# A decoder step with PEER experts on one core: top-16 lists taken in the query stage, gates placed earlier, and each gate placed by two single-pass products

## The reference, cut to what matters

```python
qry = einsum('td,de->te', xb, w_query)             # 1024 -> 8 heads x 2 halves x 128
s = einsum('thjd,jkd->thjk', qry, keys)            # 16 lists of 128 scores for each token
s_top, i_top = top_k(s, 16)                        # the best 16 of each list
cand = s_top[..0..][:, None] + s_top[..1..][None]  # sums of pairs, of one head
best, pos = top_k(cand, 16)                        # the best 16 sums: 16 experts a head
gates = softmax(best)
act = gelu(einsum('thkd,td->thk', peer_u[idx], xb))
out = einsum('thk,thkd->td', gates * act, peer_v[idx])
```

## Time and profile before

| | |
|---|---|
| median of three runs | 2429.15 us (2427.97 to 2431.12) |
| the profiled execution: its own time | 2427.98 us |
| its span | 2426.2 us |
| TensorE busy | 2295.1 us, 95% of the span |
| VectorE busy | 1560.2 us, 64% |
| ScalarE busy | 893.0 us, 37% |
| GpSimd busy | 882.0 us, 36% |
| transfers | 392.73 MB, mean 162 GB/s |

### The profile page before, as it was taken

How to read it: one execution, slowest core, us unless ns; L and a number is a source line. 1 busy time by engine, 2 the same in 40 slices (tenths; PEclk the granted TensorE clock), 3 DMA queues, 4 the chain that set the end, 5 groups by cost and what they waited for, 6 DMA issues and landing times.

```text
span 2426.2 us, 34102 instructions
## 1 busy us (share of the span) xinstructions
PE 2295.1 (95%) x12935; PEld 1956.2 (81%) x12935; DVE 1560.2 (64%) x3461; ACT 893.0 (37%) x1175; POOL 882.0 (36%) x428
## 2 busy tenths in 40 slices
PE   5999999868998999999989999999999999999998
PEld 4998899746648888888778888888888888888886
DVE  4766579464713158888889997786565555555552
ACT  3434455561122143323335554455332222222221
POOL 1333246154524337557510210000454444444441
PEclk9999999987998999999999999999999999999999
DMA  7221122646645255555546897586664555445540
GB/s 272 70 88 55 57 73 70 187 142 198 202 175 134 81 135 143 145 142 141 134 126 187 255 266 204 160 234 186 239 237 179 207 200 198 176 187 207 191 155 35
DMA packets 307412, 392.73 MB, mean 162 GB/s; under 512 B 14545, under 2 KB 257637, under 8 KB 302914
## 3 DMA queue, kind: packets, MB, share of 16 engines
q1 hardware_dynamic: 212162, 302.86, 40.3%
q10 hardware_dynamic: 91664, 75.54, 9.5%
q0 software_dynamic: 3456, 12.58, 1.6%
HBM read 305.70 MB, written 81.26 MB: 159 GB/s over the span
## 4 chain that ended last, share of the span: by engine, by line
PE 59%; DVE 3%; POOL 2%; issue 0%; ACT 0%; DMA 0%; DVEq 0%; ACTq 0%; POOLq 0%
PE bank L2597 29%; PE bank L2052 25%; PE bank L2548 4%; POOL utL_hid L2035 2%; DVE work L2271 1%; DVE work L2272 1%; PE bank L2553 1%; PE bank L2538 1%; DVE utL_hid L2042 0%; DVE ut_hid L2022 0%; DVE work L1980 0%; DVE work L1964 0%; POOL work L1964 0%; DVE work L2426 0%; PE bank L2617 0%
## 5 line engine op out<-in xcount | busy, mean ns | idle before, releaser
L2052 PE MATMUL bank<-pH,utH_hid 128*128 128x512 f32 x1024 | 406.1, 397 | 4.5 <-POOL utL_hid L2035 4.5
L2052 PE MATMUL bank<-pH,utL_hid 128*128 128x512 f32 x1024 | 400.0, 391 | 0.0
L2052 PE MATMUL bank<-pL,utH_hid 128*128 128x512 f32 x1024 | 400.0, 391 | 0.0
L2597 PE MATMUL bank<-area,work 128*128 128x512 f32 x1536 | 350.8, 389 | 0.0
L2597 PEld LDWEIGHTS bank<-area,work 128*128 128x128 f32 x1536 | 288.4, 188 | 59.7
L2209 POOL TENSOR_TENSOR work<-work,work 128x1024 fp32r<-128x1024 f32 x64 | 155.8, 2436 | 368.5 <-ACT work L2456 368.5
L2035 POOL TENSOR_TENSOR utL_hid<-ut_hid,utH_hid 128x1024 fp32r<-128x1024 f32 x66 | 182.5, 2767 | 175.8 <-PE bank L2052 147.7
L864 PE MATMUL ps_in<-hH_in,wH_in 128*128 128x260 f32 x816 | 237.4, 291 | 2.4 <-DVE projarea L915 1.4
L2370 DVE TENSOR_TENSOR utL_hid<-u_hid,utH_hid 128x512 fp32r<-128x512 f32 x64 | 147.5, 2305 | 135.3 <-ACT utH_hid L2460 135.3
L864 PE MATMUL ps_in<-hL_in,wH_in 128*128 128x260 f32 x816 | 231.8, 284 | 0.0
L864 PE MATMUL ps_in<-hH_in,wL_in 128*128 128x260 f32 x816 | 231.5, 284 | 0.0
(11 more groups left out here) (533 smaller groups left out, 4470.6 us busy)
## 6 DMA issues: line engine op xcount, KB each, us to landing
u_hid<-in_peer_u_dram SPq DMA_DIRECT2D x256, 256.0 KB, 5.0
work<-in_peer_v_dram SPq DMA_DIRECT2D x64, 1024.0 KB, 4.8
hidden_dram<-ge_hid ACTq DMA_DIRECT2D x64, 512.0 KB, 2.7
gates_dram<-area ACTq DMA_DIRECT2D x16, 2048.0 KB, 12.2
wb_in<-in_w_in_dram SPq DMA_DIRECT2D x26, 1024.0 KB, 5.1
wstage<-in_w_ada_dram SPq DMA_DIRECT2D x32, 512.0 KB, 5.0
area<-hidden_dram SPq DMA_DIRECT2D x16, 1024.0 KB
area<-gates_dram SPq DMA_DIRECT2D x16, 1024.0 KB
```

The costliest lines, as they stand in the source:

```text
L2052: mm = self.nc.tensor.matmul(self.pa[u % 2][:, :], w[:, k, :], x[:, k, :], start=(n == 0), stop=(n == 3 * KD - 1))
L2597: mm = nc.tensor.matmul(bank[k], v[s][:, j, cols], w[s][:, j, :], start=(start and x == 0), stop=(stop and x == 2))
```

## The change

It has four parts.

1. **Scores and lists move into the query stage.** After query product n TensorE scores list n-2 (4 float32 matmuls, `score`), from a copy that ScalarE now makes of each product (`evict`); ScalarE keeps the scores (`keep`), and VectorE takes the lists 0 to 12 of all four tiles there (`best_of_list`). `LATE` = 3 lists are left for units 0 to 5. The sub keys are loaded at the start of the query stage, and the first pair of expert rows at its middle; VectorE transposes that pair there.
2. **GpSimd does nothing for the units any more.** All 128 `move_low` and all picks are VectorE's.
3. **The selection of a tile has 11 steps** (`steps_by_unit`): in units 6 to 21 one step a unit, from 22 to 76 one in every second unit. Quads start in unit 19: one a unit up to 84, then 62 quads over the 37 units from 85 to 121.
4. **A gate is a rounded high part and a rest.** VectorE's one-hot carries the high part; ScalarE multiplies it by the ratio of rest to high part (`low_hots`), and TensorE adds two float32r products (`place`) where there was one float32 product. Step 10 of the selection computes the ratio, and a fourth row of `res` and `S.sel` carries it.

```diff
+            def evict(n):
+                act.wait_ge(q["product"], n + 1)
+                if n >= QR:
+                    act.wait_ge(q["scored"], n - QR + 1)
+                A_(halves(qry[n % QR]), ps[n % 2][:, :, 0:HN], ACT.Copy)
+                A_(S.qs[:, n % 2, n // 2, :], ps[n % 2][:, 1, T - HN:HN], ACT.Copy).then_inc(q["evicted"], 1)
+            def keep(n):
+                act.wait_ge(q["scored"], n + 1)
+                A_(S.lists[n], quad[n % 2], ACT.Copy).then_inc(q["kept"], 1)
             for n in range(2, CHUNKS):
                 move_high(n)
+                evict(n - 2)
+                if n >= 3:
+                    keep(n - 3)
                 if n == 3:
                     act.wait_ge(q["s_turned"], 1)
                     A_(halves(rows[:, :]), pt[0:B, :, :], ACT.Copy).then_inc(q["s_row"], 1)
+            for n in range(CHUNKS - 2, CHUNKS):
+                evict(n)
+                keep(n - 1)
+            keep(CHUNKS - 1)
...
+                    for a in range(4):
+                        sp.dma_start(S.hu[0][32 * a:32 * a + 32, :, :], S.uv[a, :, 0:8, :]).then_inc(q["first_in"], 16)
...
-            for n in range(CHUNKS):
-                dve.wait_ge(q["product"], n + 1)
-                V.tensor_copy(halves(qry[:, n, :]), ps[n % 2][:, :, 0:HN]).then_inc(q["evicted"], 1)
+            for n in range(CHUNKS - LATE):
+                dve.wait_ge(q["kept"], n + 1)
+                best_of_list(V, own, S.lists[n], S.wk, S.top[:, :, n, :], S.idx[:, :, n, :], range(NC))
...
+            def low_hots(q):
+                act.wait_ge(m["hot"], q + 1)
+                for t in range(4):
+                    last = nc.scalar.activation(oh[q % OH][:, 2, t, :], oh[q % OH][:, 0, t, :].bitcast(F32), ACT.Copy, scale=S.sel[:, 3, 4 * q + t:4 * q + t + 1])
+                last.then_inc(m["hot_low"], 1)
...
             def place(q):
-                pe.wait_ge(m["hot"], q + 1)
+                pe.wait_ge(m["hot_low"], q + 1)
...
                 for t in range(4):
-                    mm = nc.tensor.matmul(quad[q % 4][:, t, :], oh[q % OH][:, 1, t, :], oh[q % OH][:, 0, t, :], start=True, stop=True)
+                    for x in (0, 2):
+                        mm = nc.tensor.matmul(quad[q % 4][:, t, :], oh[q % OH][:, 1, t, :], oh[q % OH][:, x, t, :], start=(x == 0), stop=(x == 2))
...
             for u in range(UNITS):
-                if FIRST_DVE <= u + 1 < UNITS:
-                    H.move_low_dve(dve, u + 1)
+                if u + 1 < UNITS:
+                    H.move_low(dve, u + 1)
                 for q in QUADS[u]:
                     one_hots(q)
-                if u + 3 < UNITS and QUADS[u]:
+                if u + 3 < UNITS:
                     H.turn(dve, u + 3)
+                if u < 2 * LATE:
+                    l = 2 * PH - LATE + u // 2
+                    best_of_list(V, own, S.lists[l], S.wk, S.top[:, :, l, :], S.idx[:, :, l, :], range(2 * (u % 2), 2 * (u % 2) + 2))
+                if u in STEP:
+                    select(*STEP[u])
```

More of the change, by code:

```diff
@@ L1725, with best_of_list, query_phase @@
 UNITS = NKEY
-def query_phase(nc, A, S, XH, XL, hT, qry, PH_, PL_, buffers, sample_rows, first):
+def best_of_list(V, own, src, wk, top, idx, tiles):
+    for half in range(2):
+        at = slice(8 * half, 8 * half + 8)
+        of = wk if half else src
+        for t in tiles:
+            last = V.max(top[:, t, at], of[:, t, :])
+        own(last)
+        for t in tiles:
+            last = V.max_index(idx[:, t, at], top[:, t, at], of[:, t, :])
+            if not half:
+                last = V.match_replace(wk[:, t, :], top[:, t, at], src[:, t, :], LOW)
+        own(last)
+def query_phase(nc, A, S, XH, XL, hT, PH_, PL_, buffers, sample_rows, first):
     per = 2
@@ L1735, in query_phase @@
     BY_POOL = (2, 4, 5, 7)
+    QR = 3
+    qry = [carve(S.work, AT_OH + N * i, (P, N)) for i in range(QR)]
+    keys = carve(S.work, AT_OH + N * QR + 8, (P, 2, P))
     with Phase(nc) as ctx:
-        sb = lambda n, s: ctx.enter_context(nc.sbuf_tensor(f"{n}_query", s, F32))
         sem = ctx.sem
@@ L1825, in _, with score @@
             mm.then_inc(q["s_sum"], 1)
+            pe.wait_ge(q["keys_in"], 16)
+            nc.tensor.transpose(pk[:, 0:P], keys[:, 0, :], S.ident[:, :])
+            nc.tensor.transpose(pk[:, P:2 * P], keys[:, 1, :], S.ident[:, :]).then_inc(q["keys_t"], 1)
+            def score(n):
+                pe.wait_ge(q["evicted"], n + 1)
+                if n == 0:
+                    pe.wait_ge(q["keys_s"], 1)
+                if n == 1:
+                    pe.wait_ge(q["s_scaled"], 1)
+                if n >= 2:
+                    pe.wait_ge(q["kept"], n - 1)
+                for t in range(NC):
+                    mm = nc.tensor.matmul(quad[n % 2][:, t, :], qry[n % QR][:, t * L:(t + 1) * L], S.keysT[:, n % 2, :], start=True, stop=True)
+                mm.then_inc(q["scored"], 1)
             for n, h in [(0, 0), (1, 0), (0, 1), (1, 1)] + [(n, h) for n in range(2, CHUNKS) for h in range(2)]:
```

335 lines of the change are left out of this document (161 added, 174 removed).

## The result

| kernel | median us | range us | runs |
|---|---|---|---|
| before | 2429.1 | 2428.0 to 2431.1 | 4 |
| changed | 2468.0 | 2461.1 to 2478.8 | 4 |

The medians differ by 38.9 us, 1.6%. The recorded ratio, 1.0145 with a 95% interval of 1.0116 to 1.0175, is not quite the ratio of the medians (1.0160), but its interval holds it: the change costs some 35 to 39 us. The forecast was 2423 us with a range up to 2446, so both sign and range are missed. The profiled one took 2461.09 us, the fastest of the four; its span is 33.1 us above that of before (2426.2).

The account below looks back on a forecast made before the run. TensorE was taken as the bound nearly to the end. Query end 0.8, less 16.4 won, plus 9.0 new waits and 0.4 transposes gave -6.2 us: 2428.0 to 2421.8, median 2423, range 2408 to 2446.

Parts of the forecast that it names:

- the last sentence of part 4: Quads: ScalarE's four multiplications take about 1 us a quad on an engine busy half the time; no cost added.
- the part is worth nothing on TensorE: Quads: two float32r products give eight records like one float32 product, both bound by weight loads, 0.89 us; no gain.
- price of a record: Quads on TensorE: each record takes 0.111 us, set by its weight load, for float32 and float32r alike.
- cheap weight loads: Rival for the quads: weight loads do not bind float32r products, so about 2383 us; chance 0.06.
- four passes: Rival for the quads: narrow float32r products take float32's four passes, so about 2518 us; chance 0.12.
- Query end: Last query products to first unit: 19.0 + 2 + 2.5 = 23.5 us against 22.7, so 0.8 us slower.
- the weights of product 8: Query stage: weights land late behind the rearranging and expert rows; TensorE waits 1 to 6 us, taken as 2.
- 2.5 us of half clock in unit 0: First hidden unit: pauses behind score 15 lower TensorE's clock, losing 2.5 us (0 to 2.7).
- The early gates, the lists and VectorE: Lists hidden at 5.1 us against 6.6; VectorE falls behind in units 20 to 22, then pairs fit, 12.0 against 12.7.
- Backlog: VectorE's late one-hots make TensorE wait in units 21 to 23 and near the sample steps: 9 us of new waits.
- The forecast's terms for this stage: Hidden stage: 16.4 us of waits and half clock won, 9.0 of new waits, 0.4 for four more transposes.
- the 16.4 us that TensorE could win: Hidden stage: 13.7 us of waits for one-hots and GpSimd's rests plus 2.7 lost at half clock, all removable.

Follow-up runs that it names:

- the moved rows: Changed kernel, with SyncE issuing the four loads of the first expert rows behind the fifth pair of query weights instead of ahead of it: 2467.9 us.
- the version with all three edits: Changed kernel with one float32 product a gate, hidden-row and gate stores issued by SyncE, and first expert rows loaded behind the fifth pair of query weights: 2421.9 us.

## Why the prediction was wrong

**The step that failed** is the last sentence of part 4: "ScalarE's four multiplications a quad: 0.31 us each with overlap 0.2 to 0.3, about 1 us, on an engine busy for half of the time", costed at nothing. The length was near (four take 1.28 us, not 1), and the busy share was right (43%). What was not asked is whether ScalarE is always there to do them. It issues transfers as well, and the trace of before showed what that can take. Busy time does not count it, since an engine held in an issue is shown as idle. Moving the stores away gave 19.7 us of the hidden stage back, and 21 us of the median.

**The second term** is the same part's "the part is worth nothing on TensorE". Its price of a record held: eight records are 0.89 and 0.90 us as forecast, and the rivals of cheap weight loads and of four passes are both out. That it is the weight loads that set it was read from rows of before; no run tests it apart. The 81 ns of the Trainium skill (TensorE: Matmul & The Clock Gate, Back-to-back issue gap) would have made a quad an estimated 0.65 us; no run here shows it. But 17.7 us came beside the records: 4.4 us as 0.04 or 0.05 us a unit, 8.8 us at half clock near the samples' products, and 3.6 us of small waits, because a quad now waits for ScalarE behind VectorE (9.1 against 5.5 us). That is 16.8 of the 17.7.

**Query end.** The form was right: four scores stand behind each product, 6.62 us from product to product (6.6 forecast), the lists keep step, and the weights of product 8 are waited for. Only the size was off: the wait was 5.41 us instead of 2, and the product behind it ran at half clock, 2.0 us more. The range given was 1 to 6 us, but the clock was not in it. The forecast's 0.8 us has in it 2.5 us of half clock in unit 0, which lies behind the border taken here. Up to the border it was 19.0 + 2 - 22.7 = -1.7 us, and 3.5 was measured: 5.2 more, which the wait (3.4 more) and the clock (2.0) account for. In unit 0 the clock took 1.9 us instead of 2.5 (granted 0.81 in 864 to 874 us).

**The early gates, the lists and VectorE.** Right, nearly in place and size. Backlog cost 7.7 us for 9.0. With the other two causes taken out, the hidden stage is 843.1 us against 849.4: -6.4 by unrounded starts. The forecast's terms for this stage, with the clock in unit 0, give -16.4 + 9.0 + 0.4 + 2.5 = -4.5. With what that execution shows in their place, 5.5 us of waits for one-hots, 1.1 for VectorE's rests (after which the forecast did not ask) and 1.7 of clock, they give -7.7. So of the 16.4 us that TensorE could win some 15 were won.

**The sum.** Forecast for the profiled execution: -6.2. Found: ScalarE's stalls 19.7, two products 17.7, the rest of the hidden stage -6.4, the query stage 3.5, the stages ahead -1.9: 32.6 of 33.1. These are differences from version to version, so they must add up, and how the 37.4 us split depends on the order: with the float32 product put back first it takes 30.7 us of the hidden stage (880.5 to 849.8), and the moved stores take the other 6.7. Both edits take the multiplications' waits away. Nor is a stage the same in each execution: with the stores moved it was 860.8 and 863.7 us (only hidden rows), with the stores on ScalarE 880.5 and 888.5. The median lies 7 us above the profiled execution, where I had put it 1.2 above. The profile with the moved rows shows how stalls vary (10.8 us the longest, 25.0 us of waits), but four executions cannot settle that this is the whole of it: the kernel before, too, spread over 16 us in later comparisons, and the stages ahead vary by up to 20 us.

What stays open is why a unit with float32r quads takes 0.04 us longer, and why three of the gates' stores land so late. That the stall is 11.57 us at one place and 1.5 to 2.6 us at eight others goes with the landing (22.0 us against 8.7 to 10.4), but no run changes the landing alone. The large one at 1401 us lies where GpSimd gathers expert rows and the 16 DMA engines are busy for 0.99 of the time (window 1400 to 1420). That this is the cause isn't shown: the kernel before had 1.08 there too, and its longest stall was 4.74 us.

## What to carry to other kernels

Before an engine gets work on which the critical engine waits in each step, read what that engine does besides computing: its issues of transfers in the timeline, above all what it issues behind a large one, since an issue that is held is not busy time and the page's share doesn't show it. If it can be held, give the transfers to an engine on which nobody waits. And where float32 products are replaced by float32r ones with as many records, look at the granted clock beside other narrow products: here the count and the time of the records were equal, and the clock still fell.

## What the runs showed of the hardware that I had not expected

- The stall of a queue belongs to the issuing engine, not to the transfer. Behind 2 MB of gates it held ScalarE for 11.57 us, and with the stores moved it held SyncE for 10.63 us in issuing four loads that else take 1.79. With only the stores of hidden rows (512 KB each) moved away, ScalarE issued the 2 MB in 0.38 us and was not held. The hold ended 2.3 to 6.3 us before the gates landed, in all eleven places of the changed kernel.
- The clock fell while the records have TensorE busy for 40.00 of 40 us: granted 0.87 with float32r quads, 1.00 with float32 quads of the same record time beside the same one-column products. The Trainium skill (TensorE: Matmul & The Clock Gate, What's actually happening) has the clock follow how busy the engine has been lately. The trace's busy time does not tell these two kernels apart, so it cannot be read as that measure.
- A pause of 2.08 us ahead of product 8 was followed by half clock as one of 5.41 us was (7.53 and 7.96 us instead of 5.99). One of 1.68 us, in the version with all three edits, was not (6.00 us).
